# Sums of squares of q and k: plain fp32 products against rounded products of two halves

## The reference, cut to what matters

```
def l2_normalize(x):
    return x * lax.rsqrt(jnp.sum(x * x, axis=-1, keepdims=True) + EPS)
...
    qkv, dconv_new = causal_dwconv(qkv, dconv_prev, dn_conv_w)
    qkv = jax.nn.silu(qkv)
    q, k, v = jnp.split(qkv, [DN_KEY, 2 * DN_KEY], axis=-1)
    q = l2_normalize(q.reshape(bsz, t_len, DN_HEADS, DN_DK).astype(f32)) * (DN_DK ** -0.5)
    k = l2_normalize(k.reshape(bsz, t_len, DN_HEADS, DN_DK).astype(f32))
```

## Time and profile before

| what | value |
|---|---|
| median of 3 runs | 4511.41 us (4508.22 to 4514.65) |
| span of the profiled execution, first to last instruction | 4522.7 us |
| mean granted TensorE clock | 0.985 |
| PE busy | 4398.5 us, 97% |
| DVE busy | 3422.1 us, 76% |
| POOL busy | 1433.4 us, 32% |
| ACT busy | 1328.5 us, 29% |
| the loop over heads | 54.7 to 657.6 us of the span |

### The profile page before, as it was taken

One profiled execution on the slowest core, in us unless ns is written; L12 is line 12 of the kernel. 1 busy time (PEld: TensorE's weight loads), 2 busy tenths in 40 slices (PEclk: granted clock), 3 DMA queues, 4 the chain that ended last, 5 costly groups with the idle time before them and its releaser, 6 DMA issues. The chain is left out here.

```text
span 4522.7 us, 66871 instructions
## 1 busy us (share of the span) xinstructions
PE 4398.5 (97%) x25933; PEld 4107.4 (91%) x25933; DVE 3422.1 (76%) x4218; ACT 1328.5 (29%) x1768; POOL 1433.4 (32%) x872
## 2 busy tenths in 40 slices
PE   8999999999999999999888999999999999999997
PEld 8999999999998998999887989989989999999985
DVE  4788885434433430168988999999999999999998
ACT  4323233222221221232372222322222232323222
POOL 0111123222222333233443333333343343343342
PEclk8999999999999999999999999999999999999998
DMA  3222223222224434222289999999999999999998
GB/s 118 86 86 88 86 84 113 76 63 77 80 94 162 135 117 157 101 107 71 87 279 362 392 383 392 393 374 387 391 391 396 393 389 395 394 390 392 392 385 335
DMA packets 255165, 1084.69 MB, mean 240 GB/s; under 512 B 23601, under 2 KB 72113, under 8 KB 181425
## 3 DMA queue, kind: packets, MB, share of 16 engines
q0 software_dynamic: 74752, 538.99, 30.4%
q1 hardware_dynamic: 139824, 399.73, 25.0%
q10 hardware_dynamic: 40320, 142.10, 8.1%
HBM read 1015.85 MB, written 64.88 MB: 239 GB/s over the span
## 5 line engine op out<-in xcount | busy, mean ns | idle before, releaser
L488 PE MATMUL ps<-xhi,hi 128*128 128x320 f32 x2560 | 771.2, 314 | 10.6 <-ACT arena L853 6.5
L488 PE MATMUL ps<-xlo,hi 128*128 128x320 f32 x2560 | 759.5, 310 | 0.0
L2622 PE MATMUL ps<-xlo,whi 128*128 128x384 f32 x1984 | 665.7, 336 | 0.0
L2622 PE MATMUL ps<-xhi,whi 128*128 128x384 f32 x1984 | 664.5, 335 | 0.0
L3057 POOL DMA_INDIRECT work<-in_peer_u,sel x256 | 430.0, 1680 | 656.8 <-DVE hid L2947 631.6
L2658 PE MATMUL ps<-vhi,ahi 128*128 128x512 f32 x1488 | 590.1, 397 | 24.6 <-DVE workr L2925 24.2
L2967 DVE SCALAR_TENSOR_TENSOR keep<-work,act_w,keep 128x2048 f32<-128x2048 f32 x256 | 599.9, 2344 | 7.7 <-DMA work<-in_peer_v,sel 7.0
L3057 POOL DMA_INDIRECT work<-in_peer_v,sel x256 | 391.3, 1529 | 673.1 <-DVE keep L2967 665.8
L2947 DVE CUSTOM_DVE_ANT_0 work<-work,keep 128x2048 f32<-128x2048 f32 x256 | 584.3, 2284 | 26.0 <-DMA work<-in_peer_u,sel 24.9
L2659 PE MATMUL ps<-workr,ahi 128*128 128x512 f32 x1488 | 589.8, 396 | 0.0
L2660 PE MATMUL ps<-vhi,alo 128*128 128x512 f32 x1308 | 517.7, 396 | 0.0
(11 more groups left out here) (373 smaller groups left out, 7833.4 us busy)
## 6 DMA issues: line engine op xcount, KB each, us to landing
work<-in_v_units ACTq DMA_DIRECT2D x256, 512.0 KB
keep<-in_w_first SPq DMA_DIRECT2D x160, 512.0 KB, 3.6
work<-in_u_units SPq DMA_DIRECT2D x120, 512.0 KB
wraw<-in_u_units SPq DMA_DIRECT2D x120, 512.0 KB
keep<-in_w_units SPq DMA_DIRECT2D x32, 1024.0 KB, 5.0
gates_dram<-work SPq DMA_DIRECT2D x8, 3072.0 KB, 12.1
gbuf<-gates_dram SPq DMA_DIRECT2D x30, 768.0 KB
arena<-in_w_units SPq DMA_DIRECT2D x32, 512.0 KB, 4.0
```

The costliest lines, as they stand in the source:

```text
L488: m = pe.matmul(out[:, o:o + HT], w[:, k, :], x[:, 8 * kh + k, c], start=kh == 0 and i == 0, stop=kh == 1 and i == 23)
L2622: pe.matmul(out, h3[:, k, :], (xlo if m % 2 else xhi)[:, 8 * half + k, :], start=half == 0 and m == 0, stop=False)
```

## The change

The squares are now written twice by ScalarE: once in fp32 as before, and once in the rounded format (`sqh`). GpSimd subtracts the rounded squares from the exact ones (`sql`), behind the small copies of its iteration and ahead of the transfer of the convolution prefix. TensorE multiplies both by a rounded matrix of ones, 320 columns at a time, and sums the four products of a kind into the two halves of the same buffer. The square roots read the buffer by halves. The matrix of ones is made once, at the start, by GpSimd.

```diff
+            def sum_squares(out, i):
+                for x in (sqh, sql):
+                    for o, cols in TCOLS:
+                        m = pe.matmul(out[:, o:o + HT], ones_r[:], x[:, i, cols], start=x is sqh, stop=x is sql)
+                return m
...
-                pe.wait_ge(sq_done["q"], c + 1)
+                pe.wait_ge(sq_lo["q"], c + 1)
                 pe.wait_ge(norm_root["q"], c + 1)
-                sum_rows(ps[3], at(SQ, T)).then_inc(mm_sum["q"], 1)
-                pe.wait_ge(sq_done["k"], c + 1)
+                sum_squares(ps[3], 0).then_inc(mm_sum["q"], 1)
+                pe.wait_ge(sq_lo["k"], c + 1)
                 pe.wait_ge(evac["v"], c + 1)
-                sum_rows(ps[2], at(SQ + T, T)).then_inc(mm_sum["k"], 1)
+                sum_squares(ps[2], 1).then_inc(mm_sum["k"], 1)
...
-                    act.activation(at(SQ + i * T, T), stg[kd], ACT.Square).then_inc(sq_done[kd], 1)
+                    act.activation(at(SQ + i * T, T), stg[kd], ACT.Square)
+                    act.activation(sqh[:, i, :], stg[kd], ACT.Square).then_inc(sq_done[kd], 1)
...
-                    act.activation(at(SQ + i * T, T), ps[3 if kd == "q" else 2][:, 0:T], ACT.Sqrt, bias=epsc[:, 0:1]).then_inc(norm_root[kd], 1)
+                    act.activation(at(SQ + i * T, T).rearrange("p (a b) -> p a b", a=2), halves(ps[3 if kd == "q" else 2][:]),
+                                   ACT.Sqrt, bias=epsc[:, 0:1]).then_inc(norm_root[kd], 1)
...
+                for i, kd in enumerate("qk"):
+                    wait(sq_done[kd], c + 1)
+                    pool.tensor_tensor(sql[:, i, :], at(SQ + i * T, T), sqh[:, i, :].bitcast(F32), ALU.subtract).then_inc(sq_lo[kd], 1)
+
                 wait(cconv_done, c + 1)
```

More of the change, by code:

```diff
@@ L160, in build @@
         csum = sb("csum", [P, T])
+        sqh, sql = (sb(n, [P, 2, T], F32R) for n in ("sqh", "sql"))
+        ones_r = sb("ones_r", [P, P], F32R)
         ident = cst[:, IDENT, :]
@@ L242, in build @@
         sq_done = {kd: sem(f"sq_done_{kd}") for kd in "qk"}
+        sq_lo = {kd: sem(f"sq_lo_{kd}") for kd in "qk"}
+        ones_set = sem("ones_set")
         mm_sum = {kd: sem(f"mm_sum_{kd}") for kd in "qk"}
@@ L493, in sum_rows @@
                 return pe.matmul(out[:, NP_TOK:T], ones, src[:, NP_TOK:T], start=start, stop=stop)
+            def sum_squares(out, i):
[3 more added lines that the diff above has]
+                return m
+            pe.wait_ge(ones_set, 1)
             pe.wait_ge(x_hi, 2 * TILES)
@@ L1463, in iteration @@
                     wait(cstate_out, c * 32 + 32)
+            pool.wait_ge(ld_par, 48)
+            pool.tensor_copy(ones_r[:], ones).then_inc(ones_set, 1)
             pool.wait_ge(ld_pre, 16)
```

## The result

The changed kernel takes 4523.55 us in the median of 17 runs, the kernel before 4514.65 us in 17 runs beside them: ratio 1.0021, 95% interval [1.0015, 1.0027]. That is 0.2% slower, 8.9 us by the medians; the interval runs from 6.8 to 12.2 us. The profiled execution spans 4531.9 us; before it was 4522.7 us. It is the longest of the 17 runs (its time is 4533.43 us), so the two spans alone prove little.

The account below looks back on a forecast made before the run. The prediction took the ScalarE and VectorE circle of waits to set the period in heads 2 to 6, with TensorE slack. Squares +7.1, blocking +2.5 and head 7's sums -0.9 gave +8.7 us: 4520.1 us (+0.19%), range 4514 to 4527.

Parts of the forecast that it names:

- the blocking: In the head loop, GpSimd's running subtraction holds back VectorE's two-input SBUF instructions: 0.41 us a head at low 12, 2.5 us.
- TensorE's saving: The two sums of a head shrink from 2.08 to 1.17 us; the 0.91 us counts only in head 7.
- ScalarE's squares: Two more squares ahead of hi 12 delay VectorE by 1.19 us a head, 7.1 us over heads 1 to 6.
- the circle: Waits of ScalarE and VectorE on each other in the head loop, said to set the 75.45 us period in heads 2 to 6.
- GpSimd's subtraction: Takes 1.57 us; q's costs nothing, k's makes VectorE's low 12 lose 0.41 us a head, 2.5 us in all.
- The wait before low 12: Sign of being right: VectorE's wait for hi 12 in the loop is 2 us or more in place of 0.93.
- the waits for the evacuation of q: Sign of being right: TensorE's four waits in the loop for q's evacuation, 4.0 us, stay.
- The new waits: TensorE's waits at the sums for GpSimd's subtractions cost nothing; the first gate-stage low half is in time by a small margin.
- TensorE's saving counts: Rival: TensorE sets the loop's period, so eight heads give 7.3 us and the time is 4504.1 us; chance 4%.
- the delay is hidden: Rival: unseen slack in the loop takes up ScalarE's 1.28 us; -0.9 to +2 us, about 4511.5 us; chance 4%.
- The squares only: Rival: the subtractions never meet a VectorE instruction that matters; +6.2 us, 4517.6 us; chance 22%.
- blocks in full: Rival: k's subtraction holds VectorE's low 12 or next tap 1.57 us each head; +15.6, 4527.0 us; 18% with halfway forms.

Follow-up runs that it names:

- e2: The changed kernel with its second squares and subtractions, but TensorE sums the fp32 squares by plain products: period 77.02 us, loop 534.07 us, ratio 1.0027.
- e9: The kernel before with low 12 behind the taps of v and hi 11 ahead of the silu of q, plain sums: loop 509.33 us, ratio 0.9973.
- e10: The order of e9 with rounded sums, VectorE making the subtractions behind low 12: loop 501.43 us, 4494.38 us, ratio 0.9957 to the kernel before.
- e1: The changed kernel without GpSimd's subtraction, TensorE summing the rounded squares twice: period 76.50 us, loop 530.03 us, ratio 1.0015.
- e11: The changed kernel with the sum over k's squares repeated six times more in heads 0 to 6: loop 531.61 us, ratio 1.0014.
- e8: The changed kernel with the sum over k's squares repeated three times more in heads 0 to 6: loop 533.18 us, ratio 1.0025.
- e4: The changed kernel with second squares behind hi 12 on ScalarE and subtractions behind v's taps on VectorE: period 75.33 us, loop 521.49 us, ratio 0.9995.

## Why the prediction was right, and where it was off

The forecast was 4520.1 us (+0.19%, span 4531.4); measured were 4523.55 us, a ratio of 1.0021, and a span of 4531.9. The difference is better than its parts, and that is luck. In the loop the forecast was +8.7 us and +10.6 came. The missing 1.9 us are a term that the prediction did not have (the clock, 1.5) and one that it took too small (the blocking, 0.6), less 0.2 on the squares; the span agrees because the rest of the program came out 1.4 us shorter in that one execution. The absolute time is 3.5 us off, most of it since the kernel before measured 4514.65 us in its 17 runs and not the 4511.4 us of three. One sum of the prediction is wrong: 0.3 to 0.6 us of blocking give 4519.4 to 4521.2 us by its terms, not up to 4523.

- *TensorE's saving.* Forecast 0.91 us, in head 7 alone. Shown: 2.08 to 1.17 us in the profile, and 0.94 us once by e2. It counts eightfold only where TensorE sets the period (e9 against e10).
- *ScalarE's squares.* Forecast 1.19 us a head and 7.1 in all. Shown by e1: 1.14 and 6.9. The timeline of ScalarE had given it: a square costs its distance to the next start, and the circle had no slack behind it.
- *GpSimd's subtraction.* Forecast 0.41 us a head, 2.5 in all; measured 0.52 and 3.1. Its length was right (1.57 us). The prediction let GpSimd start 0.26 us behind q's square but only 0.14 us behind k's (275.46 to 275.6), and gave no reason; with 0.26 us for both its own sum gives 0.53 us a head. Measured were 0.27 us behind q's and 0.18 us behind k's, and VectorE was held to 0.13 us, not 0.18, before the end; held to the very end it would have lost 0.65 us. q's subtraction stretched low 11 by 0.61 us and cost nothing, as forecast.
- *The wait before low 12.* The prediction gave 2 us or more here as a sign of being right; it is 0.93 to 0.95 us in each head. Its own figures say so: with low 12 due at 276.58 and the first tap done at about 275.56 the wait is 1.0 us. Hi 12 does come 1.3 us later, but low 11 comes 0.64 us later too and is stretched by 0.61 us. The growth shows in the period and not in this wait, and where no subtraction runs (e1) the wait is 1.53 us.
- *TensorE's clock.* Not forecast: +1.5 us in head 7, shown by e11. The prediction had the longer wait (3.9 us; 2.6 to 3.9 came) and took it as free. The statement that the waits for the evacuation of q stay was wrong for the same reason: three of four are gone. In the changed kernel, e1, e2 and e8 it stands in just those of heads 2 to 6 in which the clock did not fall: the slow stretch eats that slack.
- *The new waits.* None of TensorE for a subtraction and none for the first low half of the gate stage, as forecast (it was made from 662.38 to 664.80, TensorE came at 668.26); the prefix transfer, issued at 278.91, was in time.

The sum over the loop is then 6.9 + 3.1 - 0.9 + 1.5 = +10.6 us, as measured (the 3.1 is the changed kernel's growth less e1's). Of the rivals, "TensorE's saving counts" fell by e2 and "the delay is hidden" by e1. "The squares only" and "blocks in full" lie on either side of the 0.52 us. Whether the whole time moved by more or less than 0.2% the interval does not say.

## What to carry to other kernels

An engine at 97% busy over a kernel can have slack in the stage that a change touches. Read there who waits for whom, follow the waits round until they close, and price an added instruction by whether it stands on that circle: the same arithmetic cost 10 us in one place and nothing in another (e4, where the subtractions also changed engines). A longer wait is not free for certain either: look at the granted clock behind it. If the change is right in itself but lands on the circle, shorten the circle first; then its saving counts.

## What had not been expected of the hardware

The granted clock of TensorE fell to half behind waits as short as 1.98 us, in 18 of 22 cases, for a stretch in which matmuls of 320 columns start 0.27 us apart instead of 0.146. In head 7 this took the time from the first q unit to the sums from 70.5 us (585.00 to 655.51) to 72.0 (595.05 to 667.09). And a GpSimd subtraction of 640 columns takes 1.57 us with two different inputs, but 1.28 us in the median when both inputs are the same tile.
